# Down projection of routed experts as three split passes, with the hand-written order of an expert pair rearranged

## The reference, cut to what matters

```python
def swiglu(x, w_gate, w_up, w_down):
    return (jax.nn.silu(x @ w_gate) * (x @ w_up)) @ w_down

def body(acc, blk):
    tok, w, e = blk
    xb = x_pad[tok]
    yb = swiglu(xb, w_gate[e], w_up[e], w_down[e]) * w[:, None]
    return acc.at[tok].add(yb), None
```

## Time and profile before

| | us |
|---|---|
| median of 3 runs | 1889.63 |
| profiled execution, its own time | 1890.4 |
| its span in the profile | 1888.6 |
| TensorE busy (PE) | 1721.7, 91% of the span |
| VectorE busy (DVE) | 968.7, 51% |
| ScalarE busy (ACT) | 794.5, 42% |
| GpSimd busy (POOL) | 559.5, 30% |
| mean granted clock of TensorE | 0.967 of full |

### The profile page before, as it was taken

How to read it: one execution, slowest core, us unless ns; L and a number is a source line. 1 busy time by engine, 2 the same in 40 slices (tenths; PEclk the granted TensorE clock), 3 DMA queues, 4 the chain that set the end, 5 groups by cost and what they waited for, 6 DMA issues and landing times. The chain is left out here.

```text
span 1888.6 us, 24985 instructions
## 1 busy us (share of the span) xinstructions
PE 1721.7 (91%) x7154; PEld 1077.1 (57%) x7155; DVE 968.7 (51%) x1594; ACT 794.5 (42%) x1480; POOL 559.5 (30%) x742
## 2 busy tenths in 40 slices
PE   6999999987986699999999998999999999879887
PEld 4666666544774465666566655566666566544343
DVE  3333343314997354555455446445455354637994
ACT  2222222212331355666555547455565555743222
POOL 0000011000655232333323224233233233424551
PEclk9999999987998799999999999999999999989899
DMA  9200000021111787788777669768688676958761
GB/s 362 101 0 0 0 0 0 15 97 47 68 67 52 258 297 252 272 282 310 248 259 258 231 226 317 241 237 288 223 295 289 228 270 225 325 207 335 284 201 39
DMA packets 124129, 363.76 MB, mean 193 GB/s; under 512 B 29078, under 2 KB 44374, under 8 KB 121501
## 3 DMA queue, kind: packets, MB, share of 16 engines
q1 hardware_dynamic: 88021, 290.85, 44.3%
q0 software_dynamic: 35760, 72.49, 10.8%
q10 hardware_dynamic: 320, 0.07, 0.0%
HBM read 334.52 MB, written 71.91 MB: 215 GB/s over the span
## 5 line engine op out<-in xcount | busy, mean ns | idle before, releaser
L1413 PE MATMUL Y<-raw_d,hT 128*128 128x512 f32 (+1 forms) x768 | 351.4, 601 | 19.7 <-ACT hT L1473 19.7
L198 DVE TENSOR_TENSOR lo_gu<-raw_g,hi_gu 128x1024 fp32r<-128x1024 f32 x130 | 153.5, 1220 | 364.7 <-ACT hi_gu L191 297.0
L1371 PE MATMUL GU<-hi_gu,x_hi 128*128 128x512 f32 (+1 forms) x768 | 322.0, 419 | 5.9 <-issue 4.2
L1371 PE MATMUL GU<-hi_gu,x_lo 128*128 128x512 f32 (+1 forms) x768 | 304.8, 397 | 0.0
L1371 PE MATMUL GU<-lo_gu,x_hi 128*128 128x512 f32 (+1 forms) x768 | 304.2, 396 | 0.0
L1332 POOL DMA_INDIRECT y_dram<-y,to_row x128 | 131.3, 1026 | 470.1 <-ACT y L1481 352.2
L1481 ACT ACTIVATE y<-Y,w_t 128x512 f32<-128x512 f32 (+1 forms) x256 | 168.3, 683 | 237.0 <-PE Y L1413 232.0
L1413 PEld LDWEIGHTS Y<-raw_d,hT 128*128 128x128 f32 (+1 forms) x768 | 131.9, 178 | 178.6 <-issue 167.1
L1321 POOL DMA_INDIRECT rows<-rows_dram,from_row x131 | 160.0, 1221 | 109.1 <-POOL from_row L1319 79.3
L1371 PEld LDWEIGHTS GU<-hi_gu,x_hi 128*128 128x128 f32 (+1 forms) x768 | 136.7, 178 | 77.5 <-issue 39.5
L1371 PEld LDWEIGHTS GU<-lo_gu,x_hi 128*128 128x128 f32 (+1 forms) x768 | 135.9, 177 | 47.1 <-issue 9.3
(11 more groups left out here) (224 smaller groups left out, 2090.8 us busy)
## 6 DMA issues: line engine op xcount, KB each, us to landing
raw_g<-in_w_exp_gate SPq DMA_DIRECT2D x130, 512.0 KB, 6.0
raw_u<-in_w_exp_up SPq DMA_DIRECT2D x130, 512.0 KB, 6.3
raw_d<-in_w_exp_down SPq DMA_DIRECT2D x130, 512.0 KB, 4.4
yk<-y_dram SPq DMA_DIRECT2D x16, 2048.0 KB, 12.3
rows_dram<-row SPq DMA_DIRECT2D x9, 512.0 KB, 2.7
h_dram<-resid SPq DMA_DIRECT2D x9, 512.0 KB, 2.7
res<-h_dram SPq DMA_DIRECT2D x9, 512.0 KB, 4.6
w_big<-in_w_in SPq DMA_DIRECT2D x2, 2048.0 KB, 12.2
```

The lines of the kernel that those rows point to most:

```text
L198: dve.tensor_tensor(part_of(keep, "lo", m, par, h), part_of(keep, "raw", m, par, h), part_of(keep, "hi", m, par, h).bitcast(F32), ALU.subt ...
L1371: ins = pe.matmul(out, lhs[x], rhs[w], start=first and i == 0, stop=last and i == 2)
L1413: ins = pe.matmul(Y[half][0:n, :], hT[b][:, f, :], raw_d[par][:, f, cols], start=f == 0, stop=f == FC - 1)
```

## The change

The down product becomes three split passes: raw_d now has one buffer, and ScalarE and VectorE make hi_d and lo_d of it (one buffer each) in the pair in which they are used; the hidden rows are split into hT_hi and hT_lo (h_low is a new instruction on VectorE). ScalarE applies Silu to the gate, so that hidden is one multiplication. In two_blocks, transposes(1, m) stands first, then both gate_up, then h_transposes(0) and transposes(0, m+1); in one_block h_transposes(0) stands ahead of transposes(0, m+1). ScalarE's and VectorE's lists are rearranged, and the last weighted half of block 1 moves to VectorE. The weight queue loads g0, u0, g1, u1, d0, d1, with the d halves behind their low parts. The load of g_final moves into the output stage. Semaphores are renamed and their start values changed to fit (not shown).

```diff
@@ experts, weight queue
-                for name in "gu":
-                    for h in range(2):
+                for h in range(2):
+                    for name in "gu":
                         sp.wait_ge(lo_set[name], 2 * m + h + 1)
...
                 for h in range(2):
-                    sp.wait_ge(y_done[1], 2 * m + 1)
-                    sp.dma_start(part_of(keep, "raw", "d", 1 - par, h), expert_weights(a, "d", e, h)).then_inc(
+                    sp.wait_ge(lo_set["d"], 2 * m + h + 1)
+                    sp.dma_start(part_of(keep, "raw", "d", 0, h), expert_weights(a, "d", e, h)).then_inc(
@@ experts, GpSimd, scatter
-                pool_after(pool, keep["passed"], y_ev[1], 2 * m + b + 2)
+                for half in range(2):
+                    pool_after(pool, keep["passed"], y_ev[half], 2 * m + b + 2)
@@ experts, TensorE
-            def down(b, m, par, half, counts):
+            def down(b, m, half, counts):
                 n = BLK[b]
-                pe.wait_ge(h_ev[b], m + 2)
+                pe.wait_ge(h_lo_ev[b], m + 2)
                 pe.wait_ge(y_ev[half], 2 * m + b + 1)
                 cols = slice(half * 512, (half + 1) * 512)
                 for f in range(FC):
                     if b == 0 and half == 0:
-                        pe.wait_ge(ld["d"][f], 16 * m + 16)
-                    ins = pe.matmul(Y[half][0:n, :], hT[b][:, f, :], raw_d[par][:, f, cols], start=f == 0, stop=f == FC - 1)
+                        pe.wait_ge(lo_set["d"], 2 * m + f + 1)
+                    ins = three(Y[half][0:n, :], (hT_hi[b][:, f, :], hT_lo[b][:, f, :]),
+                                (hi_d[:, f, cols], lo_d[:, f, cols]), f == 0, f == FC - 1)
                 ins.then_inc(y_done[half], counts)
 
             def two_blocks(m, par):
+                transposes(1, m)
                 gate_up(0, m, par)
-                transposes(1, m)
+                gate_up(1, m, par)
+                h_transposes(0, m)
                 transposes(0, m + 1)
-                h_transposes(0, m)
-                gate_up(1, m, par)
-                down(0, m, par, 0, 1)
+                down(0, m, 0, 1)
                 h_transposes(1, m)
-                down(0, m, par, 1, 1)
-                down(1, m, par, 0, 1)
-                down(1, m, par, 1, 1)
+                down(0, m, 1, 1)
+                down(1, m, 0, 1)
+                down(1, m, 1, 1)
@@ one_block
                 gate_up(0, m, par)
+                h_transposes(0, m)
                 transposes(0, m + 1)
-                h_transposes(0, m)
-                down(0, m, par, 0, 2)
-                down(0, m, par, 1, 2)
+                down(0, m, 0, 2)
+                down(0, m, 1, 2)
@@ experts, ScalarE
-                act.activation(sig[b][0:BLK[b], :], GU[b][0:BLK[b], 0:FE], ACT.Sigmoid).then_inc(sig_ready[b], 1)
+                act.activation(silu[b][0:BLK[b], :], GU[b][0:BLK[b], 0:FE], ACT.Silu).then_inc(silu_ready[b], 1)
...
+            def down_high(m, h):
+                act.wait_ge(y_done[1], 2 * m + 1)
+                split_hi(act, keep, "d", m, 0, h)
+
             def pair(m, par):
+                x_high(1, m)
+                down_high(m, 0)
+                down_high(m, 1)
                 for name in "gu":
-                    for h in range(2):
-                        split_hi(act, keep, name, m + 1, 1 - par, h)
-                sigmoid(0, m)
-                x_high(1, m)
+                    split_hi(act, keep, name, m + 1, 1 - par, 0)
+                gate(0, m)
+                h_high(0, m)
                 x_high(0, m + 1)
-                h_high(0, m)
-                sigmoid(1, m)
+                for name in "gu":
+                    split_hi(act, keep, name, m + 1, 1 - par, 1)
+                gate(1, m)
                 weighted(0, m, 0)
                 h_high(1, m)
                 weighted(0, m, 1)
                 weighted(1, m, 0)
-                weighted(1, m, 1)
@@ experts, VectorE
-                own.did(dve.tensor_tensor(hid[b][0:n, :], sig[b][0:n, :], GU[b][0:n, 0:FE], ALU.mult))
-                own.wait()
-                dve.tensor_tensor(hid[b][0:n, :], hid[b][0:n, :], GU[b][0:n, FE:2 * FE], ALU.mult).then_inc(h_ready[b], 1)
+                dve.tensor_tensor(hid[b][0:n, :], silu[b][0:n, :], GU[b][0:n, FE:2 * FE], ALU.mult).then_inc(h_ready[b], 1)
+
+            def h_low(b, m):
+                n = BLK[b]
+                dve.wait_ge(h_hi_ev[b], m + 1)
+                dve.tensor_tensor(hT_lo[b][:].rearrange("p f q -> p (f q)"), GU[b][:, 0:FC * n],
+                                  hT_hi[b][:].rearrange("p f q -> p (f q)").bitcast(F32),
+                                  ALU.subtract).then_inc(h_lo_ev[b], 1)
+
+            def weighted(b, m, half):
+
+                dve.wait_ge(y_done[half], 2 * m + b + 2)
+                dve.wait_ge(y_ev[half], 2 * m + b + 1)
+                dve.wait_ge(y_st[b], 16 * m + 16)
+                dve.sem_inc(passed, 1)
+                dve.tensor_scalar(y[b][0:BLK[b], half * 512:(half + 1) * 512], Y[half][0:BLK[b], :],
+                                  w_t[0:BLK[b], b, bass.ds(m, 1)], None, ALU.mult).then_inc(y_ev[half], 1)
 
             def pair(m, par):
+                x_low(1, m)
                 for h in range(2):
-                    split_lo(dve, keep, "g", m + 1, 1 - par, h)
-                split_lo(dve, keep, "u", m + 1, 1 - par, 0)
+                    split_lo(dve, keep, "d", m, 0, h)
+                for name in "gu":
+                    split_lo(dve, keep, name, m + 1, 1 - par, 0)
                 hidden(0, m)
-                x_low(1, m)
+                h_low(0, m)
                 x_low(0, m + 1)
-                split_lo(dve, keep, "u", m + 1, 1 - par, 1)
+                for name in "gu":
+                    split_lo(dve, keep, name, m + 1, 1 - par, 1)
                 hidden(1, m)
-                own.clear()
+                h_low(1, m)
+                weighted(1, m, 1)
@@ output, weight queue
             hidden(2)
+            sp.dma_start(g_fin[:], a["g_final"].rearrange("(a d) -> a d", a=1).broadcast_to([P, D])).then_inc(keep["output_ld"], 16)
             hidden(3)
```

More of the change, by code:

```diff
@@ L131, in build @@
             **{f"{m}_ld{h}": sem(f"{m}_ld{h}") for m in "gud" for h in range(2)},
-            **{f"{part}_set_{m}": sem(f"{part}_set_{m}") for m in "gu" for part in ("hi", "lo")},
+            **{f"{part}_set_{m}": sem(f"{part}_set_{m}") for m in "gud" for part in ("hi", "lo")},
         )
@@ L136, in mid @@
                 return middle.enter_context(nc.sbuf_tensor(name, shape, dt))
-            keep |= dict(raw_g=mid("raw_g", [P, KC, FE]), raw_u=mid("raw_u", [P, KC, FE]), raw_d=[mid("raw_d0", [P, FC, D])])
+            keep |= dict(raw_g=mid("raw_g", [P, KC, FE]), raw_u=mid("raw_u", [P, KC, FE]), raw_d=mid("raw_d", [P, FC, D]))
             with ExitStack() as front:
@@ L150, in build @@
                 router(nc, a, c, keep, rows_dram, h_dram, list_dram)
-            for name, shape in (("ple", [P, TILES, PLE]), ("g_ple", [P, D]), ("g_fin", [P, D])):
+            for name, shape in (("ple", [P, TILES, PLE]), ("g_ple", [P, D])):
                 keep[name] = ctx.enter_context(nc.sbuf_tensor(name, shape, F32, side="right"))
@@ L180, in part_of @@
     if m == "d":
-        return keep["raw_d"][par][:, h, :]
+        return keep[f"{kind}_d"][:, h, :]
     k = slice(h * (KC // 2), (h + 1) * (KC // 2))
@@ L252, in mixer @@
         rden = sb("rden", [P, HEADS])
-        late = keep["raw_d"][0][:].rearrange("p f d -> p (f d)")
+        late = keep["raw_d"][:].rearrange("p f d -> p (f d)")
         vc = late[:, 0:SEQS * KV].rearrange("p (b k) -> p b k", b=SEQS)
@@ L1228, in experts @@
         keep["lo_gu"].append(sb("lo_gu1", [P, 2, KC, FE], F32R))
-        keep["raw_d"].append(sb("raw_d1", [P, FC, D]))
-        hi_gu, lo_gu, raw_d = (keep[n] for n in ("hi_gu", "lo_gu", "raw_d"))
+        keep["hi_d"] = sb("hi_d", [P, FC, D], F32R)
+        keep["lo_d"] = sb("lo_d", [P, FC, D], F32R)
+        hi_gu, lo_gu, hi_d, lo_d = (keep[n] for n in ("hi_gu", "lo_gu", "hi_d", "lo_d"))
         x_hi = [sb(f"x_hi{b}", [P, KC, BLK[b]], F32R) for b in range(2)]
         x_lo = [sb(f"x_lo{b}", [P, KC, BLK[b]], F32R) for b in range(2)]
-        hT = [sb(f"hT{b}", [P, FC, BLK[b]]) for b in range(2)]
+        hT_hi = [sb(f"hT_hi{b}", [P, FC, BLK[b]], F32R) for b in range(2)]
+        hT_lo = [sb(f"hT_lo{b}", [P, FC, BLK[b]], F32R) for b in range(2)]
         rows = [sb(f"rows{b}", [P, D]) for b in range(2)]
         y = [sb(f"y{b}", [P, D]) for b in range(2)]
-        sig = [sb(f"sig{b}", [P, FE]) for b in range(2)]
+        silu = [sb(f"silu{b}", [P, FE]) for b in range(2)]
         from_row = [sb(f"from_row{b}", [P, 1], I32) for b in range(2)]
@@ L1306, in _ @@
                 sp.wait_ge(gate_ld, 16 * E * r + 16 * E)
-                sp.sem_inc(sp_passed, 1)
-            sp.wait_ge(keep["output_ld"], 16 * 4)
+                sp.sem_inc(passed, 1)
```

(13 more changed lines are left out.)

29 lines of the change are left out of this document (14 added, 15 removed).

## The result

| | before | after |
|---|---|---|
| median of 4 runs, us | 1889.72 | 2040.43 |
| span of the profiled execution, us | 1888.6 | 2037.6 |
| experts' stage, us | 1050 | 1199 |
| mean granted clock | 0.967 | 0.930 |

The account below looks back on a forecast made before the run. TensorE was taken to bound the experts' stage, with written-order waits deciding: two-block experts +56, one-block +34 and -9, sum +81; falling clock +54; together +135 us on 1890.4, so 2025 us, range 1985 to 2065.

Parts of the forecast that it names:

- Two-block experts: Experts with two blocks: 22.0 us against 20.24, +1.8 each, 32 times, +56 us before any loss of clock.
- The walk: Following TensorE, ScalarE and VectorE through one expert in written order; sum over all experts +81 us.
- G+6.02: Two-block expert: h_transposes(1) 6.02 us after G, when TensorE has finished gate_up(1), behind a new wait of about 2.9 us.
- One-block experts: Behind a one-block expert 14.2 us against 11.96, 15 times, +34 us; behind a two-block one 11.2 against 11.7, -9 us.
- 1.3 for the clock: One-block behind one-block: a 4.3 us pause lowers the clock, costing 1.3 us each, 15 times, 20 us.
- The clock: Pauses lower TensorE's clock; in two-block experts 1.6 us in two of three, 34 us; together with one-block ones +54.
- Rival (a): The walks hold but the clock stays up: +81, 1971 us; chance 0.31.
- The down product: TensorE's three split passes start 0.23 us apart, 0.46 behind the pause; 73 us less work for TensorE.
- the table loads: Possible ScalarE function loads of 1.28 us in the experts' loop: taken as nothing, 20 us put into the upper end.
- GpSimd is off the chain: Edits costed at nothing: the scatter waits on both weighted halves, but GpSimd's work was said to hold up nothing.
- The weight queue: Weight loads in order of use, each waiting on a low half done most of an expert earlier: costed at nothing.
- Rival (b): Hidden(1) is ready in time, TensorE stays full and its 73 us are gained: about 1816 us; chance 0.07.

Follow-up runs that it names:

- the last run: Three-pass kernel with TensorE's old two-block order, no table loads and branches on ScalarE and VectorE, plus first u split moved behind next expert's x: 1835.35 us.
- the second run, run 2: Changed kernel with gate(1) right behind gate(0) on ScalarE and hidden(1) right behind hidden(0) on VectorE: 1947.47 us.

## Why the prediction was right

The forecast was 2025 us, the measured time 2040, on the side and by the mechanism that were forecast. The ends of its range, 1985 and 2065, are the sums 1989 and 2062 rounded outwards.

- **Two-block experts.** The walk gave a pause of 2.9 us and h_transposes(1) at G+6.02; it came at G+5.66 after 2.69 us. ScalarE and VectorE went hand in hand a little closer than the rows of before have it (h_high at G+0.42 instead of 0.6). Time at the full clock 22.0 foretold, 22.1 to 22.2 measured. That the order makes the pause is shown by the run that moves two instructions of each expert (-93 us); the run with TensorE's old order (-112 us) has no such pause either. That the two gate/up in a row are behind it is the walk's reading: no run moves them alone.
- **One-block experts.** 14.2 foretold behind a one-block one and 1.3 for the clock, 15.5 together; 13.83 in six of 15 and 14.85 on the mean, or 14.03 without table loads: by this count 1.3 for the clock was too much. The four low halves ahead of hidden(0) are in the trace. That they set the time is shown by the last run, where one fewer brought 33 us, in a kernel with branches and the old order; in the changed kernel itself it was not tried. 0.93 us is the least wait for the hidden product that a one-block expert behind a one-block one has in any run with three passes.
- **The clock.** 1.6 us in two of three two-block experts, 34 us, was an estimate from pauses of 2.70 and 2.71 us. Filling the pauses gave 35: by the starts of the experts some 29 of it in the two-block ones, 5 in the one-block ones behind them. In the cases that can be compared, 10 of 15 fell, by 1.2 us each, so the term was right in sum and a little high in each case. The two in three was taken from two pauses; that it held is luck. Rival (a), that the clock stays up, falls.
- **The down product.** Passes start 0.23 us apart, as foretold, where the clock is up, and 0.43 where it is down (0.46 foretold).
- **By kind of expert.** In the two timelines, from TensorE's first instruction of one expert to that of the next, over 61 of the 64 (a wait for gathered rows counts to the expert that waits), two-block experts cost 94 us more than before (90 foretold) and one-block ones behind a one-block one 54 more (54 foretold). Those behind a two-block one cost 1 less: the forecast was 9 less, since the walk had them at 11.7 before and 11.2 after, where the traces have 11.42 and 11.35. That the 54 came out is luck: without the table loads the same 15 experts cost 40, so the walk and the clock were some 14 too high, and the loads, costed at nothing, made up for it.
- **Costed at nothing, and not nothing.** Two steps. "GpSimd is off the chain" failed for the gather: transposes(1, m) moved from behind gate_up(0) to the head of the expert, past 5.5 us of cover, and waited 11.8 us in five experts; with the old order these waits are gone. Behind the three longest (3.1 to 4.0 us) some twelve gate/up passes ran at the lower clock (granted 0.53 from 960 to 966, behind the first of them), which cost some 2.4 us more each time. And the table loads, taken as nothing with 20 us in the upper end, came, at the head of the pass and a second time ahead of Silu: 9 us. Without them the one-block experts took some 16 us less and the two-block ones, waiting longer for gathered rows, some 8 more. The Trainium skill ("ScalarE activation tables: per-element evaluation and per-set limits", section "Table sets in the compiler and the runtime") says that loads are placed block by block, for the longest run. What I drew from that, one load at the head of each pass, was nearer than my reading of the trace of before, whose loop begins and ends with the same function; the second load I had from neither, and the price was 9 us, not the 22 that I put on it. These two steps, 9 and 12 us, are more than the 15 that the forecast was short; the one-block terms that were too high hide the rest. The weight queue was rightly costed at nothing: ScalarE waits for no weight load in the stage.
- **Rival (b)**, TensorE full and 1816 us: what it needs was built in the end, and its gain is real (1835), but with branches and an order that the change did not have.

## What to carry to other kernels

When TensorE bounds a stage by its share, ask for each step that it is given earlier who has to answer it, and what stands ahead of the answer in that engine's list: here, by the walk, two products put side by side moved one hand-over out from under them, and everything behind it in two other lists waited too. Before taking work off the bounding engine by giving it to others, walk one unit of the loop in list order for every kind of unit and every predecessor; the busy shares of VectorE and ScalarE (50 and 57% of the stage) would have promised the opposite sign. A pause costs more than its length where the clock falls behind it.

## What was not expected of the hardware

- Ten passes that nobody needs made the kernel 35 us faster, since TensorE then stood still for 0.38 us in place of 2.69. With the same pause the clock fell in 10 of 15 comparable experts and stayed in 5; after the 0.91 us pauses of the second run 2 to 2 was the same within 0.05 us each time.
- The changed loop, which is entered with another function than the Silu it ends with, has two table loads per pass, one of them ahead of a plain copy; the loop before, entered and left with Sigmoid, has none. Each load took 1.28 us of ScalarE; one dummy Silu ahead of the loop took all 64 away.
